# A two-layer transformer block on one core: the dilated attention passes reordered by head pairs, with each pair's combination inside them

## The reference, cut to what matters

```python
# second block, h = rmsnorm(x), proj = h @ w_in
# three groups g: (window, dilation) = (128, 1), (512, 4), (2048, 16); 8 heads of 64 features each
for g, (window, dilation) in enumerate(DILATED_GROUPS):
    q = partial_rope(qkv[:, :, 0, g], positions)      # the first 16 of 64 features are rotated
    k = partial_rope(qkv[:, :, 1, g], positions)
    o, lse = dilated_attention(q, k, qkv[:, :, 2, g], window, dilation)
alpha = softmax(stack(lses), axis=0)                  # over the three groups
attn = sum(alpha[..., None] * stack(outs), axis=0)
# spatial gate: z = gelu(uv); u, v = halves of 512 features
v = layernorm(v, ln_g, ln_b)
mixed = einsum('gts,bnsgc->bntgc', tril(w_s), chunks_of_128(v)) + b_s
sgu = u * mixed
merged = gate_a * (attn @ w_proj_attn) + gate_b * (sgu @ w_proj_sgu)
# first block's feed-forward part, right before: ff = square(relu(h @ w_ff1)) @ w_ff2
```

## Time and profile before

| | us |
|---|---|
| median of 3 runs | 3688.54 |
| runs | 3684.5 to 3690.34 |
| the profiled execution's own time | 3685.35 |
| its span | 3683.5 |
| TensorE busy | 3530.9 (96%) |
| VectorE busy | 1454.4 (39%) |
| GpSimd busy | 1045.7 (28%) |
| ScalarE busy | 976.9 (27%) |
| mean granted clock of TensorE | 0.978 of full speed |

### The profile page before, as it was taken

One profiled execution on the slowest core, in us unless ns is written; L12 is line 12 of the kernel. 1 busy time (PEld: TensorE's weight loads), 2 busy tenths in 40 slices (PEclk: granted clock), 3 DMA queues, 4 the chain that ended last, 5 costly groups with the idle time before them and its releaser, 6 DMA issues.

```text
span 3683.5 us, 45040 instructions
## 1 busy us (share of the span) xinstructions
PE 3530.9 (96%) x17659; PEld 2929.1 (80%) x17659; DVE 1454.4 (39%) x2358; ACT 976.9 (27%) x1629; POOL 1045.7 (28%) x473
## 2 busy tenths in 40 slices
PE   7899999999989999999799999987999999999999
PEld 6788877888777888888678888886787778888887
DVE  6882452123345333333644444447123213122234
ACT  4233443222242111111333333333322221111112
POOL 1452102222215333333333233321232222232222
PEclk9999999999999999999899999978999999999999
DMA  4232012212311111111211111122222111111111
GB/s 134 54 93 76 30 50 66 65 55 69 114 75 58 46 46 53 50 46 43 106 52 33 46 46 47 47 94 95 66 74 85 58 52 46 46 46 57 46 46 57
DMA packets 194267, 226.88 MB, mean 62 GB/s; under 512 B 19112, under 2 KB 165204, under 8 KB 193500
## 3 DMA queue, kind: packets, MB, share of 16 engines
q1 hardware_dynamic: 178556, 169.85, 15.2%
q10 hardware_dynamic: 11776, 46.63, 3.5%
q0 software_dynamic: 3808, 8.64, 0.7%
HBM read 191.30 MB, written 31.69 MB: 61 GB/s over the span
## 4 chain that ended last, share of the span: by engine, by line
PE 85%; issue 8%; DVE 4%; POOL 1%; ACT 1%; DMA 1%; ACTq 0%; DVEq 0%; POOLq 0%
PE ps L270 18%; PE ps L315 16%; PE ps L297 13%; PE ps L298 13%; PE ps L291 12%; PE ps L720 4%; PE ps L2535 2%; POOL wlo L262 1%; PE ps L2523 1%; PE ps L2121 1%; PE ps L2506 1%; PE ps L2102 1%; PE ps L2504 1%; PE ps L331 1%; DVE big L466 0%
## 5 line engine op out<-in xcount | busy, mean ns | idle before, releaser
L262 POOL TENSOR_TENSOR wlo<-raw,whi 128x2048 fp32r<-128x2048 f32 (+1 forms) x162 | 701.5, 4330 | 1728.3 <-ACT whi L254 1727.4
L297 PE MATMUL ps<-h_lo,whi 128*128 128x512 f32 x1856 | 724.5, 390 | 0.5 <-POOL wlo L262 0.4
L298 PE MATMUL ps<-h_hi,wlo 128*128 128x512 f32 x1856 | 723.4, 390 | 0.0
L254 ACT ACTIVATE whi<-raw 128x2048 fp32r<-128x2048 f32 (+1 forms) x162 | 288.4, 1780 | 969.4 <-PE ps L291 599.2
L291 PE MATMUL ps<-h_hi,whi 128*128 128x512 f32 x1856 | 464.7, 393 | 20.9 <-ACT fr L936 13.9
L291 PEld LDWEIGHTS ps<-h_hi,whi 128*128 128x128 f32 x1856 | 351.2, 190 | 95.0 <-ACT fr L936 12.4
L297 PEld LDWEIGHTS ps<-h_lo,whi 128*128 128x128 f32 x1856 | 349.8, 188 | 74.9 <-POOL wlo L262 1.9
L298 PEld LDWEIGHTS ps<-h_hi,wlo 128*128 128x128 f32 x1856 | 349.7, 188 | 72.7
L1045 DVE TENSOR_TENSOR big<-big,ps 128x512 f32<-128x512 f32 x432 | 296.1, 687 | 251.8 <-PE ps L270 251.6
L315 PE MATMUL ps<-h_lo,whi 128*128 128x512 f32 x880 | 351.8, 400 | 1.8 <-POOL wlo L262 1.8
L270 PE MATMUL ps<-whi,f_hi 128*128 128x512 f32 x864 | 337.9, 391 | 6.6 <-DVE big L1045 6.5
(11 more groups left out here) (336 smaller groups left out, 4970.9 us busy)
## 6 DMA issues: line engine op xcount, KB each, us to landing
raw<-in_w_ff_dram SPq DMA_DIRECT2D x32, 1024.0 KB, 5.1
raw<-in_w_in_dram SPq DMA_DIRECT2D x57, 512.0 KB, 4.3
raw<-in_w_in_dram SPq DMA_DIRECT2D x28, 1024.0 KB, 5.3
raw<-in_w_ffn_gate_dram SPq DMA_DIRECT2D x11, 1024.0 KB, 5.3
raw<-in_w_ffn_up_dram SPq DMA_DIRECT2D x11, 1024.0 KB, 5.2
raw<-in_w_ffn_down_dram SPq DMA_DIRECT2D x11, 1024.0 KB, 4.8
yt<-y_keep ACTq DMA_DIRECT2D x20, 512.0 KB, 3.9
raw<-in_w_out_dram SPq DMA_DIRECT2D x8, 1024.0 KB, 5.0
```

Of the source, the lines that this page charges most:

```text
L254: nc.scalar.activation(whi[c % 2][:, 0:cols], raw[c % 2][:, 0:cols], ACT.Copy).then_inc(s_hi.sem, 1)
L262: nc.gpsimd.tensor_tensor(wlo[c % 2][:, 0:cols], raw[c % 2][:, 0:cols], whi[c % 2][:, 0:cols].bitcast(F32), ALU.subtract).then_inc(s_lo.se ...
L297: nc.tensor.matmul(ps[:, bank + n, :], w(0, k, m * P, P), src[1][:, k, sl], start=False, stop=False)
L298: last = nc.tensor.matmul(ps[:, bank + n, :], w(1, k, m * P, P), src[0][:, k, sl], start=False, stop=k == ks - 1)
```

## The change

Dilated passes run pair by pair: pass i is group i % 3 and pair i // 3. When the three groups of a pair are done, its rows are loaded back (`load_pair`, ScalarE's queue, last quarter of pass 3c + 3) and combined in 13 VectorE operations on whole pairs during the next two passes, turned on TensorE, copied to `YC` by ScalarE and stored by GpSimd's queue; the fourth pair's combination stays in the gate's stage. Rotated Q and K stay in F32, and a score multiplies them once. The gate's V is projected in the free slots of passes 10 and 11, and copied raw to `gv`; its gelu, 8 instructions of 128 x 512, opens the next stage, `SpatialGate`, which takes the place of CombineAndGate. ScalarE's queue loads the fourth pair there ahead of the eleven table loads (`wsp`, `lng`, `lnb`, eight of `bsp`). Normalising takes two operations per tile, the mixed tiles are kept in `SG` and multiplied by U tile by tile, and chunks 0 to 3 are mixed between U tiles. The rope tables are computed after the first feed-forward stage's `ups(0)`.

```diff
             def slots(self, e, ups, down, after_first=None):
                 ups(0, None, [unit_no(self.u + j) for j in range(self.g)])
+                if after_first is not None and not self.onto_x:
+                    after_first(e)
...
             def act(self, e):
                 self.begin(e)
                 e.dma_start(gpb[:, :], self.gain.partition_broadcast(P)).then_inc(d_gain.sem, 16)
-                if not self.onto_x:
-                    self.rope_act(e)
...
-                self.slots(e, ups, down)
+                self.slots(e, ups, down, self.rope_act)
...
             def dve(self, e):
                 self.begin(e)
-                if not self.onto_x:
-                    self.rope_dve(e)
...
-                self.slots(e, ups, down)
+                self.slots(e, ups, down, self.rope_dve)
...
-                return (1, 4, 8)[i // 4]
+                return (1, 4, 8)[i % 3]
...
+            def gate_tile(self, i, j):
+                return 12 * (i - 10) + j - 8 if i == 11 or (i == 10 and j >= 8) else -1
+            def pair_at(i, k):
+                return (i - k) // 3 - 1 if i >= 3 + k and (i - k) % 3 == 0 else None
+            def load_pair(self, e, c):
+                if c:
+                    e.wait_ge(d_yd.sem, 16 * c)
+                for g in range(NDIL):
+                    e.dma_start(XC[:, g]..., scratch["dil_keep"][g, c]...).then_inc(pair_loaded.sem, 16)
+            def pair_weighted(self, e, c, g):
+                x = self.pair_rows(g)
+                nc.vector.tensor_tensor(x, x, cw[:, 1, 16 * g:16 * g + 16]...to_broadcast([P, 16, HD]), ALU.mult)
+            def pair_second(self, e, c):
+                self.pair_weighted(e, c, 1)
+                nc.vector.tensor_tensor(self.pair_rows(0), self.pair_rows(0), self.pair_rows(1), ALU.add)
...
# Dilated.act, per quarter q (b = 2q):
-                rounded(i, n) ...
+                        gate_tile(i, 3 * q)
                         take_turned(i, b)
                         exps(i, b + 2)
+                        if q == 3 and self.pair_at(i, 0) is not None:
+                            self.load_pair(e, self.pair_at(i, 0))
+                        if q == 2 and self.pair_at(i, 1) is not None:
+                            self.pair_exps(e, self.pair_at(i, 1))
+                        gate_tile(i, 3 * q + 1)
                         take_turned(i, b + 1)
+                        gate_tile(i, 3 * q + 2)
                         exps(i, b + 3)
+                        if q == 0:
+                            if v:
+                                split_v(i + 2)
+                            else:
+                                split_hi(e, unit_no(self.u + 2 * self.N + i - 10))
+                        if q == 2 and v:
                             split_qk(i + 2)
+                        if q == 2 and not qk:
+                            split_hi(e, unit_no(self.u + 2 * self.N + 2))
+                        if q >= 2 and self.pair_at(i, 2) is not None:
+                            self.pair_features(e, self.pair_at(i, 2), q - 2, 6)
...
# Dilated.dve, at the end of each quarter:
+                        if c is not None and q == 1:
+                            self.pair_largest(e, c)
+                        if c is not None and q == 2:
+                            self.pair_shares(e, c)
+                            self.pair_weighted(e, c, 0)
+                        if c is not None and q == 3:
+                            self.pair_second(e, c)
+                        if q == 0 and self.pair_at(i, 2) is not None:
+                            self.pair_third(e, self.pair_at(i, 2))
...
# Dilated.pe
                     for h in range(2):
-                        nc.tensor.matmul(o[h], QH[d[h], i % 2, q], KH[d[h], i % 2, k], start=False, stop=False)
-                    for h in range(2):
-                        nc.tensor.matmul(o[h], QH[d[h], i % 2, q], KL[d[h], i % 2, k], start=False, stop=False)
-                    for h in range(2):
-                        last = nc.tensor.matmul(o[h], QL[d[h], i % 2, q], KH[d[h], i % 2, k], start=False, stop=True)
+                        last = nc.tensor.matmul(o[h], QR[d[h], i % 2, q], KR[d[h], i % 2, k], start=False, stop=True)
                         last.then_inc(scores.sem, 1)
...
+                    if b == 6 and self.pair_at(i, 2) is not None:
+                        e.wait_ge(ct_taken.sem, self.ctk + 2 * self.pair_at(i, 2) + 1)
...
+                        if q >= 2 and self.pair_at(i, 2) is not None:
+                            self.turn_pair(e, self.pair_at(i, 2), q - 2, 6)
...
# SpatialGate.act
+                self.begin(e)
+                self.dilated.load_pair(e, 3)
...
+                for t in range(8):
+                    nc.scalar.activation(gv[:, t, :], gv[:, t, :], ACT.Gelu)
+                split_hi(e, unit_no(self.u + 1))
+                u_tile(0)
+                e.wait_ge(dv.sem, self.eps)
+                nc.scalar.activation(mv[:, :, 2:3], mv[:, :, 2:3], ACT.Sqrt)
+                for n in range(1, 4):
+                    u_tile(n)
+                self.dilated.pair_exps(e, 3)
+                u_tile(4)
...
# SpatialGate.pe
+                feature_tiles(e, unit_no(self.u), KT, H, 0, ..., pe_a, after=turn_mixing)   # turns the mixing weights after tile 1
+                feature_tiles(e, unit_no(self.u + 1), KT, H, 0, ..., pe_a, after=mixed)     # mixes 4 chunks after tiles 1 and 3
+                for half in range(2):
+                    self.dilated.turn_pair(e, 3, half, half)
```

More of the change, by code:

```diff
@@ new lines, in pair_third, with turn_pair @@
+            def pair_third(self, e, c):
+                self.pair_weighted(e, c, 2)
+                e.wait_ge(pair_step.sem, self.ps + 13 * c + 12)
+                nc.vector.tensor_tensor(ct[:, :, :, :].rearrange("p t h n -> p (t h) n"), self.pair_rows(0), self.pair_rows(2),
+                                        ALU.add).then_inc(pair_step.sem, 1)
+            def turn_pair(self, e, c, half, bank):
+                e.wait_ge(pair_step.sem, self.ps + 13 * (c + 1))
+                for t in range(4):
+                    last = nc.tensor.transpose(ps[:, bank, t * P:(t + 1) * P],
+                                               ct[:, 4 * half + t, :, :].rearrange("p h n -> p (h n)"), ident)
+                last.then_inc(ct_turned.sem, 1)
@@ L2341, in pool @@
             def pool(self, e):
[L2343 to L2348 removed]
                 def store(i, b):
[L2351 removed]
+                    g = i % 3
@@ L2383, in pool @@
+                    for b in range(1, 5):
+                        store(i, b)
+                    if i + 2 < self.N:
+                        split_lo(e, self.qk_unit(i + 2))
+                    if i + 1 == self.N:
+                        split_lo(e, unit_no(self.u + 2 * self.N + 2))
                     for b in (5, 6, 7):
                         store(i, b)
+                    if self.pair_at(i, 2) is not None:
+                        self.store_pair(e, self.pair_at(i, 2))
             def dve(self, e):
@@ L2570, in pe @@
                             turn_v(i + 1, q)
[L2572 to L2591 removed]
+                        if q >= 2 and self.pair_at(i, 2) is not None:
+                            e.wait_ge(p_taken.sem, self.pt + 8 * i + b + 2)
+                            self.turn_pair(e, self.pair_at(i, 2), q - 2, 6)
@@ new lines, in mixed @@
+                def mixed(n):
+                    if n % 2:
+                        for c in range(2 * n - 2, 2 * n + 2):
+                            mix(c)
+                feature_tiles(e, unit_no(self.u), KT, H, 0,
+                              lambda n: [(gv_taken, dil.gt + 15 + n)] if n < 2 else [(probs, dil.p + 8 * dil.N)], pe_a, after=turn_mixing)
+                feature_tiles(e, unit_no(self.u + 1), KT, H, 0, lambda n: [(act_a, self.aa + 8 + n + 1)], pe_a, after=mixed)
+                for half in range(2):
+                    e.wait_ge(act_a.sem, self.aa + 8 + 5 + half)
+                    dil.turn_pair(e, 3, half, half)
@@ L2815, in hybrid_kernel @@
         ff = add(FeedForward([A["w_ff1"][0]], A["w_ff2"][0], DFF, mixed.rows, Rows("ff", V_NORM + 4 * KT), A["g_post_mlp"]))
-        add(Dilated(ff.rows))
-        add(CombineAndGate())
+        dilated = add(Dilated(ff.rows))
+        add(SpatialGate(dilated))
         merge = add(Merge(A["w_in_2"][0], [O2_GA, O2_GB], [A["w_proj_attn_2"][0], A["w_proj_sgu_2"][0]], None))
```

432 lines of the change are left out of this document (188 added, 244 removed).

## The result

| | before | after |
|---|---|---|
| median of 4 runs, us | 3686.52 | 3654.70 |
| runs, us | 3683.76 to 3690.34 | 3654.13 to 3656.55 |
| span of the profiled execution, us | 3683.5 | 3654.6 |
| mean granted clock of TensorE | 0.978 | 0.985 |

The ratio is 0.9914, with a 95% interval of 0.9897 to 0.9931. The kernel is 31.8 us faster by the medians and 28.9 by the two profiled spans. The forecast was 3682.8 us (5.7 us faster), its range 3662 to 3704; the changed kernel's median lies 7 us under that range.

What follows compares the result with a forecast made beforehand. TensorE, busy 96% of the span, was taken to bound the kernel. Terms +3.5, +15.8, -15.5, -15.9 and +6.4 sum to -5.7 us, giving 3682.8 us against a median of 3688.54; range 3662 to 3704.

Steps and rivals of the forecast that it cites:

- Step 1: First FeedForward: with the rope tables moved, TensorE's idle time moves to before the down unit; +3.5 us (-2 to +7).
- Step 2: Scores in Dilated: one F32 matmul per head takes three slots, 0.645 us for 0.345 at 256 columns; +15.8 us.
- Step 3: Passes 10 and 11, with the gate's V tiles as fillers: 103.3 us for 118.8, a 4.0 us idle time included; -15.5 us.
- Step 4: Gate stage, first U tile to Merge: 68.6 us for 84.5, with 7.5 us idle before the mixing weights' transposes; -15.9 us.
- Step 5: Pairs 0 to 2 combined inside passes: transposes 2.4 us, three bank waits of 1.0, VectorE 1; +6.4 us.
- F32 heads wholly side by side: Rival for the scores: two slots instead of three, 3.7 us in place of 15.8, total 3670.7 us; chance 0.14.
- the rope wait goes: Rival in the first FeedForward: the wait truly disappears, -13.8 us in place of +3.5, total 3665.5 us; chance 0.10.
- VectorE becomes the late engine: Slower rival in the passes: pair operations blocked beside GpSimd's splits delay TensorE, 18 us, total 3700.8 us; chance 0.21.
- wide scores at 0.63: Sign against the forecast: two-chunk scores' heads at 0.63 us, where 0.83 or so was expected.

Runs made afterwards that it cites:

- rope tables back: Changed kernel with the rope tables back at the start of the first feed-forward stage; 3653.89 us.
- the order alone: Kernel before with only the passes put in the order of pairs; 3683.67 us against 3688.30, ratio 0.9994.
- The first experiment: Kernel before with each score's head as one plain F32 matmul in place of three float32r ones; 3686.62 us against 3685.23, ratio 1.000.
- that experiment: Changed kernel with the second gate V unit's split put at the end of pass 10; 3649.72 us.
- the second experiment: Changed kernel with both heads of a score taken from the first head's 64 rows; 3684.30 us, 29.6 more than the changed kernel.

## Why the prediction was wrong

Against the profiled executions the sum had to be -28.9 us, and was -5.7.

| step of the prediction | forecast | measured | from |
|---|---|---|---|
| 1 rope tables | +3.5 | +2.1 | rope tables back, two traces |
| 2 F32 scores | +15.8 | +0.2 | the score alone; 0.63 and 0.42 us |
| 3 passes 10 and 11 | -15.5 | -18.3 | 101.55 - 118.78 = -17.2; 1.5 of the pair and -0.4 of the scores stand in steps 5 and 2 |
| left out: passes 0 to 9 in the new order | 0 | -3.6 | the order alone |
| 4 gate stage | -15.9 | -16.0 | 68.5 for 84.5 |
| 5 pairs 0 to 2 | +6.4 | +4.5 | 47.10 - 45.62 in passes 5 and 8, taken for pass 11 too |
| not listed | | +2.2 | the remainder; see below |
| sum | -5.7 | -28.9 | |

The 45.62 us are a pass of dilation 8 of the changed kernel that turns no pair (pass 2). Of the unlisted 2.2 us, 0.6 lie ahead of TensorE's first instruction, 0.4 between that and Dilated outside step 1's stretch, 1.3 around pass 0, 0.5 in passes 1 to 9, and -0.6 behind the start of Merge. The 1.3 is mostly chance: it is the low clock behind the 2.8 us wait for `VF`, and two later kernels had the same wait there and lost nothing.

**Step 2 failed, and with it the forecast.** It is 15.6 of the 23.2 us between forecast and measurement. It took the duration of an F32 instruction rightly (0.215 us at 256 columns) and then counted three slots, because the second head stands behind both instructions of the first. The first experiment shows that the change of the score alone is a tie, the second that in shared rows each further slot costs 0.215 us wide and 0.105 narrow. Two slots and the switches between whole array and row halves make 0.63 us. This was the second rival, *F32 heads wholly side by side*, to which I gave 0.14; its mechanism was right and even its price of 3.7 us was too high, since it left the narrow scores at no gain (they gained 0.06 us each, 52 of them); step 2 itself had named -3 us for the case in which they gain too, and the 0.2 lies between the two. The rule of the Trainium skill, TensorEngine Tiling (Array Packing), Theoretical Speedup, was read rightly there, and the runs agree with it for F32 in row halves: 1.06 us in shared rows, 0.63 in separate ones. I had two hints in my own rows: in float32r the heads already ran side by side, and in F32 a matmul in column halves cost 0.053 us, half of 0.107. I let the order in the program outweigh that.

**Step 3 compared unlike passes.** It set passes 10 (dilation 4) and 11 (dilation 8) of the new order against two of dilation 8 and charged the difference, but never credited passes 0 to 9 with it. With that, 3.6 us were lost in arithmetic. It also took a pass in the middle as the base of pass 11. A middle pass holds the first two scores of the pass after it (0.77 us each, 2275.89 to 2276.66) and two turnings of V (0.41, 2323.35 to 2323.76 shows such four transposes), 2.4 us that pass 11 has not. It took 51.1 us for the 55.6 of steps 3 and 5 (53.5 and 2.1); 0.6 of the difference is the pair's, 0.5 the narrow scores', and 1.0 stays open. Pass 10 took 50.45 us for 49.8, with the 1.0 us wait for V in it. The wait in pass 11, 3.96 us for 4.0, was right, and the 1.8 us charged for the clock behind it fits: with the wait taken out the stretch lost 5.4 us against the changed kernel's trace, 1.5 more than the wait, and 2.4 to 2.6 more than it against the two other traces named with that experiment.

**Step 1** had the mechanism, its place (12.37 us for 11) and the sign; the down unit began at 1137.50 for 1136.3, and since this trace is 1.1 us later already at the last transposes ahead (1095.93 for 1094.81), that is the forecast's time. What was too large is the part behind it: VectorE's first addition started at 1144.30, less those 1.1 us 1143.2, for 1144.6. The rival *the rope wait goes* fell, as did *VectorE becomes the late engine*: no wait for VectorE arose in passes 3 to 9, whose lengths are those of their dilation to within 1.5 us.

**Step 4** was right in the sum, and in its parts: 8.27 us for 7.5, and Merge 68.5 us behind the first U tile, of which 5.28 are the wait for VectorE's products. **Step 5** had three waits of 1.0 us for the bank and measured some 0.5 each; a pair costs 1.5 us for 2.1.

Of what would have shown the forecast wrong, "wide scores at 0.63" came true to the digit. The range was too narrow because the three faster cases (side by side, the missing 3.6, the shorter last pass) were held one by one or not at all; they came together.

## What to carry to other kernels

When two matmuls use separate row halves, count the slots of one of them. This is shown here at 64 rows each, for float32r issued in turn and for F32 issued one head after the other; other types and orders were not run. A run with both in the same rows gives the price of a slot. When an order is changed, set the whole sequence against the whole sequence: comparing only the ends loses what the middle gained. Work moved out of the way of one wait can stand in the way of the next, so list the next deadlines of every engine whose queue it joins: against the change's place, where the rope tables cost 2 us, they gave 4 us back behind the roundings of the second up unit and 14 behind those of the third.

## What the runs showed that was not expected

A narrow score became shorter with F32 (0.42 us for 0.48) while a wide one became longer (0.63 for 0.55). The kernel before's timeline of TensorE shows why:

```profile
2172.51 0.28 PE L2508 MATMUL ps<-KL,QH 64*128 64x128 f32 x2
2172.62 0.28 PE L2510 MATMUL ps<-KH,QL 64*128 64x128 f32 x2
...
2180.73 0.29 PE L2508 MATMUL ps<-KL,QH 64*128 64x256 f32 x2
2180.85 0.28 PE L2510 MATMUL ps<-KH,QL 64*128 64x256 f32 x2
```

A further pair of float32r matmuls takes 0.11 us at 128 columns and 0.12 at 256: half the columns save 0.01 us. An F32 slot takes 0.105 and 0.215 (the second experiment). So at 128 columns two F32 slots are shorter than three float32r pairs, at 256 longer. The forecast had both lengths of float32r in its rows and priced the narrow score at +0.05 us, for its third slot.

Taking the V tiles out of the passes made the gate stage 3.0 us shorter, though nothing in that stage was changed. In the changed kernel its loads start when the last stores have landed, 4.9 us behind the first U tile; with sixteen V tiles between the last stores and the stage that wait is over, and they start 1.5 us behind it.

The same wait did not cost the same clock each time: behind 2.8 us of idle in pass 0 the mean granted clock up to pass 1 was 0.94, 0.97 or 1.00 in executions of the same instructions, 59.6, 58.8 or 57.3 us.
